# MLP up projection: the high weights meet low and high tokens in one 512-column product, and VectorE adds the halves

## The reference, cut to what matters

```python
D_MODEL = 1024
D_FF = 4 * D_MODEL

def squared_relu_mlp(x, w_up, w_down):
    return jnp.square(jax.nn.relu(x @ w_up)) @ w_down

def first_block(...):
    for layer in range(DEPTH):          # DEPTH = 2
        ...
        h = layer_norm(DEEPNORM_ALPHA * h + mix, ln1_g[layer], ln1_b[layer])
        h = layer_norm(DEEPNORM_ALPHA * h + squared_relu_mlp(h, w_up[layer], w_down[layer]),
                       ln2_g[layer], ln2_b[layer])
```

## Time and profile before

| | us |
|---|---|
| median of 3 runs | 1464.77 |
| lowest, highest | 1459.92, 1467.07 |
| profiled execution: span, first to last instruction | 1461.4 |

### The profile page before, as it was taken

One profiled execution on the slowest core, in us unless ns is written; L12 is line 12 of the kernel. 1 busy time (PEld: TensorE's weight loads), 2 busy tenths in 40 slices (PEclk: granted clock), 3 DMA queues, 4 the chain that ended last, 5 costly groups with the idle time before them and its releaser, 6 DMA issues.

```text
span 1461.4 us, 19665 instructions
## 1 busy us (share of the span) xinstructions
PE 1326.6 (91%) x6493; PEld 946.6 (65%) x6493; DVE 952.8 (65%) x2289; ACT 551.2 (38%) x1133; POOL 379.2 (26%) x384
## 2 busy tenths in 40 slices
PE   8999999999999999999998889787897989788888
PEld 6988999988988999977787535343343535343333
DVE  4687555564657555585785777776767777776755
ACT  4553544444545444454672222222222212222221
POOL 1104000000000000012642454335444354345440
PEclk9999999999999999999999999899999999999999
DMA  9615655535315555564403999999999999999997
GB/s 364 260 54 125 226 184 183 190 144 231 115 44 173 187 181 192 168 218 132 154 28 118 415 420 421 420 422 421 422 422 421 422 421 421 420 421 422 421 422 310
DMA packets 97535, 406.86 MB, mean 278 GB/s; under 512 B 6955, under 2 KB 44524, under 8 KB 60748
## 3 DMA queue, kind: packets, MB, share of 16 engines
q0 software_dynamic: 39552, 276.60, 46.0%
q1 hardware_dynamic: 57932, 129.60, 25.8%
HBM read 404.84 MB, written 1.07 MB: 278 GB/s over the span
## 4 chain that ended last, share of the span: by engine, by line
PE 50%; DMA 23%; issue 13%; DVE 10%; POOL 2%; ACT 2%; DVEq 0%; POOLq 0%; SPq 0%; ACTq 0%; PEldq 0%
DMA ring<-in_peer_uv,prob 20%; PE ps L688 13%; PE ps L689 12%; PE ps L690 12%; PE ps L841 6%; DMA uv_gain<-in_peer_uv,prob 2%; DMA ring<-in_peer_wq 1%; PE ps L815 1%; PE ps L877 1%; DVE prob L2417 1%; DVE prob L2405 1%; POOL small L1656 1%; PE ps L635 1%; DVE ring L2541 1%; DVE sco L2430 0%
## 5 line engine op out<-in xcount | busy, mean ns | idle before, releaser
L1876 DVE TENSOR_TENSOR w_low<-ring,w_high 128x1024 fp32r<-128x1024 f32 x140 | 165.2, 1222 | 151.3 <-ACT w_high L1220 150.8
L1220 ACT ACTIVATE w_high<-ring 128x1024 fp32r<-128x1024 f32 x142 | 142.7, 1052 | 171.8 <-PE ps L690 171.8
L688 PE MATMUL ps<-hT_high,w_high 128*128 128x256 f32 x512 | 145.0, 283 | 0.9 <-DVE hT_low L1869 0.9
L689 PE MATMUL ps<-hT_low,w_high 128*128 128x256 f32 x512 | 144.9, 283 | 0.0
L690 PE MATMUL ps<-hT_high,w_low 128*128 128x256 f32 x512 | 144.8, 283 | 0.0
L1471 ACT ACTIVATE prob<-prob 128x4 f32<-128x4 f32 (+2 forms) x67 | 13.8, 206 | 346.6 <-DVE prob L2541 346.6
L1459 ACT ACTIVATE sco<-const,prob 128x128 f32<-128x128 f32 x256 | 84.3, 392 | 151.7 <-DVE prob L2551 137.8
L841 PE MATMUL ps<-arena_v,sco 128*128 128x512 f32 x256 | 121.5, 619 | 18.6 <-ACT sco L1459 18.6
L1662 POOL TENSOR_SCALAR small<-small 128x1 f32<-128x1 f32 x8 | 4.3, 533 | 502.0 <-ACT arena_v L1252 502.0
L841 PE MATMUL ps<-ring,sco 128*128 128x512 f32 x192 | 102.4, 684 | 31.4 <-ACT sco L1459 31.4
L841 PE MATMUL ps<-arena_u,sco 128*128 128x512 f32 x256 | 115.7, 601 | 8.3 <-ACT sco L1459 8.3
(11 more groups left out here) (446 smaller groups left out, 3083.8 us busy)
## 6 DMA issues: line engine op xcount, KB each, us to landing
ring<-in_w_up SPq DMA_DIRECT2D x32, 1024.0 KB, 5.5
ring<-in_w_down SPq DMA_DIRECT2D x32, 1024.0 KB, 4.9
qkring<-in_qk_a SPq DMA_DIRECT2D x8, 1024.0 KB, 7.1
qkring<-in_qk_b SPq DMA_DIRECT2D x8, 1024.0 KB, 4.8
ring<-in_peer_wq SPq DMA_DIRECT2D x8, 1024.0 KB, 9.2
ring<-in_w_in SPq DMA_DIRECT2D x8, 860.0 KB, 5.5
ring<-in_w_out_a SPq DMA_DIRECT2D x4, 1024.0 KB, 15.8
ring<-in_v_b SPq DMA_DIRECT2D x4, 1024.0 KB, 7.2
```

What stands on the lines that cost most here:

```text
L688: pe.matmul(dst, a[0], b[0], start=start, stop=False, skip_group_check=True)
L689: pe.matmul(dst, a[0], b[1], start=False, stop=False, skip_group_check=True)
L1220: sc.activation(w_split[pair][0][:, part], ring[:, slot, part], ACT.Copy)\
L1876: ve.tensor_tensor(w_split[pair][1][:, part], ring[:, slot, part], w_split[pair][0][:, part].bitcast(F32), ALU.subtract)\
```

## The change

1. `hT_low` and `hT_high` become the two halves of one buffer, `hT_both`, at the same place in memory.
2. PSUM banks 4 to 7 become one tensor, `ps_up`; `ps[4]` to `ps[7]` are its slices. Each piece's up now takes two banks, one for each block of 128 hidden units: banks 4 and 5 for b = 0, 6 and 7 for b = 1.
3. In `up`, high weights times low tokens and high weights times high tokens are one matmul of 512 moving columns, which fills a bank: the low tokens' part in columns 0 to 255, the high tokens' in 256 to 511. Low weights times high tokens is added to the second half with a 256-column matmul. A group of three matmuls is now two.
4. ACT, after `up_ready`, first copies the first halves of the two banks into `relu` (a Copy in place of the Relu), and only then splits weights. DVE adds the second halves onto that, then computes max(x, 0)·x into `act_sq` with one scalar_tensor_tensor, signals `act_squared`, and then makes the weights' low halves. ACT makes `act_high` as a copy of `act_sq` after its weight split; DVE ends with `act_low` as before.
5. In the last step `final_split` now stands behind ACT's wait for `up_ready` and its copy.

```diff
-            hT_low = split("hT_low", [P, NB, S])
-            hT_high = split("hT_high", [P, NB, S])
+            hT_both = split("hT_both", [P, 2, NB, S])
+            hT_low, hT_high = hT_both[:, 0, :, :], hT_both[:, 1, :, :]
...
-        ps = [ctx.enter_context(nc.psum_tensor(f"ps{i}", [P, HALF], F32)) for i in range(8)]
+        ps = [ctx.enter_context(nc.psum_tensor(f"ps{i}", [P, HALF], F32)) for i in range(4)]
+        ps_up = ctx.enter_context(nc.psum_tensor("ps_up", [P, 4, HALF], F32))
+        ps += [ps_up[:, i, :] for i in range(4)]
...
-                        last = product(ps[4 + b][:, fb * S:(fb + 1) * S], [x[:, at:at + P] for x in w_split[pair]],
-                                       [x[:, c, :] for x in (hT_high, hT_low)], start=(c == 0), stop=(c == NB - 1))
+                        high, low = (x[:, at:at + P] for x in w_split[pair])
+                        pe.matmul(ps_up[:, 2 * b + fb, :].rearrange("p (a s) -> p a s", a=2), high, hT_both[:, :, c, :],
+                                  start=(c == 0), stop=False, skip_group_check=True)
+                        last = pe.matmul(ps_up[:, 2 * b + fb, S:2 * S], low, hT_high[:, c, :], start=False,
+                                         stop=(c == NB - 1), skip_group_check=True)
...
+                    sc.wait_ge(sem("up_ready"), count.take("up_ready"))
+                    sc.activation(relu[:, b, :].rearrange("p (f s) -> p f s", f=2), ps_up[:, 2 * b:2 * b + 2, 0:S], ACT.Copy)\
+                        .then_inc(sem("relu_ready"), 1)
                     if first:
-                        split_high(2 * b + 1, 0, "up_ready")
+                        split_high(2 * b + 1, 0)
                     elif more:
-                        split_high(2 - 2 * b, 1, "up_ready")
+                        split_high(2 - 2 * b, 1)
                     else:
                         final_split()
-                        sc.wait_ge(sem("up_ready"), count.take("up_ready"))
-                    sc.activation(relu[:, b, :], ps[4 + b][:, :], ACT.Relu).then_inc(sem("relu_ready"), 1)
-                    sc.wait_ge(sem("relu_ready"), count.take("relu_ready"))
-                    sc.activation(act_high[:, b, :], relu[:, b, :], ACT.Square).then_inc(sem("act_high"), 1)
+                    sc.wait_ge(sem("act_squared"), count.take("act_squared"))
+                    sc.activation(act_high[:, b, :], act_sq[:, b, :], ACT.Copy).then_inc(sem("act_high"), 1)
...
+                    ve.wait_ge(sem("relu_ready"), count.take("relu_ready"))
+                    pre = relu[:, b, :].rearrange("p (f s) -> p f s", f=2)
+                    then(ve.tensor_tensor(pre, ps_up[:, 2 * b:2 * b + 2, S:2 * S], pre, ALU.add))
+                    then(ve.scalar_tensor_tensor(out=act_sq[:, b, :], in0=relu[:, b, :], scalar=0.0, in1=relu[:, b, :],
+                                                 op0=ALU.max, op1=ALU.mult))
+                    ve.sem_inc(sem("act_squared"), 1)
                     if first:
                         split_low(2 * b + 1, 0)
...
-                    ve.wait_ge(sem("relu_ready"), count.take("relu_ready"))
-                    then(ve.tensor_tensor(act_sq[:, b, :], relu[:, b, :], relu[:, b, :], ALU.mult))
                     ve.wait_ge(sem("act_high"), count.take("act_high"))
```

More of the change, by code:

```diff
@@ L1387, in out_and_mlp @@
                 grow_residual()
-                with count.loop(N_CHUNK // 2 - 1, up_ready=2, relu_ready=2, w0_used=2, raw0_landed=16, raw1_landed=16,
+                with count.loop(N_CHUNK // 2 - 1, up_ready=2, act_squared=2, w0_used=2, raw0_landed=16, raw1_landed=16,
                                 raw2_landed=16, raw3_landed=16):
@@ L2095, in out_and_mlp @@
                 step(0, first=True)
-                with count.loop(N_CHUNK // 2 - 1, w_high=8, relu_ready=2, act_high=2, v_chain=2):
+                with count.loop(N_CHUNK // 2 - 1, w_high=8, relu_ready=2, act_high=2, v_chain=4):
                     step(1)
```

## The result

| | before | after |
|---|---|---|
| median, us | 1464.68 | 1469.49 |
| mean of 18 and 20 executions (standard error), us | 1463.7 (0.6) | 1469.5 (0.5) |
| profiled execution, span, us | 1461.4 | 1470.7 |

The ratio is **1.0043**, 95% interval 1.0032 to 1.0054 (1.0040 by the two means): the change makes the kernel about 6 us slower. The means leave out disturbed executions (4107.86 and 6595.08 us among the 20 before, which the median of 1464.68 counts, and in the experiments one of 2627 us before and one of 1641 us of e9). I had forecast 1465.0 and a shift of +0.2 us. What lies around a span is 1.8 us in every execution (the profiled one: 1472.5 against 1470.7).

The account below looks back on a forecast made before the run. PE was taken to bound the kernel, busy throughout both MLP windows. Terms of -4.9, 0, 0 and +5.1 us summed to +0.2 us, taking the median from 1464.8 to 1465.0 us; range 1460.0 to 1470.0.

Parts of the forecast that it names:

- Part 2: A step of the MLP loop: the down behind each up hides the new DVE and ACT work; cost 0.
- Part 3: First piece of each MLP: the longer chain to act_low stays covered by 0.2 us; cost 0, at worst 0.3 us.
- Part 4: Last piece of each MLP: nothing covers the chain, PE waits 2.5 us for act_low; +5.1 us for both.
- Part 1: The up matmuls: a group falls from 359.4 to 349.8 ns, saving 9.6 ns in each of 512, 4.9 us.
- the lower bound: Smallest expected saving in the up matmuls: 6.7 ns per group, 3.4 us, with the joined matmul at 232.9 ns.
- 1.3 us by my estimate from its rule: Rival for the up matmuls: only 2.5 ns fixed part saved per dropped matmul, giving 1468.6 us; chance 0.07.
- The clock: Rival: PE's clock falls in the new end gaps, 1.8 us per fall, 1466.8 or 1468.6 us; chance 0.25.
- a wait of PE is paid in full: In the MLPs, where PE is always busy, any wait of PE lengthens the kernel; the sum charged 2.5 us each.
- the last of the signs of failure: The forecast fails if the end gaps set off longer lower-clock stretches in the stages behind them; no size given.
- the rival with two falls: A clock fall in the end gap of both MLPs, giving 1468.6 us; one or two falls had chance 0.25.
- the 0.5% that I gave 0.87: Whole kernel: the time stays within about 0.5% (7.3 us), what a measurement can tell from no change; chance 0.87.

Follow-up runs that it names:

- e9: The changed kernel with 12 extra matmuls, results unread, filling PE's wait at the end of each MLP; mean 1465.6 us, ratio 1.0012 to before.
- e8: The changed kernel itself, unaltered, timed again on one chip beside its filled versions; mean 1468.9 us, ratio 1.0034 to before.
- e10: The changed kernel with 6 extra matmuls, results unread, half filling PE's wait at the end of each MLP; mean 1466.3 us, ratio 1.0019 to before.
- e2: The kernel before with only the final split moved late, three matmuls per group and the Relu kept; mean 1468.8 us, ratio 1.0040 to before.
- e3: The changed kernel with 12 extra unread matmuls in each end wait, first timing, on another chip than the changed kernel's; mean 1465.7 us, ratio 1.0019 to before.
- e1: The changed kernel with the final split put back ahead of the waits on ACT and DVE; mean 1462.4 us, ratio 0.9995 to before.
- e11: The kernel of e1 with three of the second last piece's matmuls moved ahead of the wait for act_ready; mean 1461.8 us, ratio 0.9993 to before.
- e5: The kernel of e1 with six of the second last piece's matmuls moved ahead of the wait for act_ready; mean 1462.3 us, ratio 0.9997 to before.

## Why the prediction was wrong

**Right.** What bounds the kernel, and that only the fixed part of a matmul can be saved. Part 2: PE busy for 120.00 of 120 us, ups and downs without a wait for `w_low`. Part 3: no wait of PE at the first piece (`act_low` ends at 155.88, 0.3 us before PE wants it at 156.15; the forecast was 0.2). Part 4: one wait of PE in each MLP, 12 matmuls after the last up, with the final low halves right ahead of `act_low`; that it cancels what the loops win was the core of the forecast, and it does, and takes 2.1 us more (5.8 against 3.7).

**Part 1, mis-sized.** 9.6 ns a group was 6.5: 3.3 us instead of 4.9 over 512 groups. I had chosen the down's 230.0 ns because it stands next to the up in time. The nearer row by kind was the output projection's 232.9, where tokens are an operand as well; it gave 3.4 us as the lower bound. That this is close to the 3.3 us measured is luck: the joined matmul takes 236.1 ns, 3.2 more than the row, and the 256-column one behind it 116.8, 3.0 less than the 119.8 that I had kept. By stages the loops win 3.7 us, since the downs run a shade faster too. The Trainium skill ("TensorE: Matmul & The Clock Gate", "Back-to-back issue gap") would have had 1.3 us by my estimate from its rule; the fixed parts of 23 and 10 ns above the columns (236.1 - 213.3, 116.8 - 106.7) don't agree with its 2.5.

**Part 4, mis-sized.** 2.5 us each was 3.1 and 2.7: 5.8 instead of 5.1 us. Of it 0.1 us each is the hand-over from DVE to PE, and 0.4 us at the first MLP is DVE, which starts the low halves at 315.08 though `act_sq` ended at 314.57 and the first high half at about 314.1. It does so in every trace of the changed kernel, filled or not, at the first MLP and in none at the second. Each time it starts 0.06 us behind the end of ACT's second high half (315.02 in this trace), though by the code it waits only for the first; why, I don't know.

**The clock, the step that failed.** I named it as a rival at 0.25 and left it out of the sum. The sum took "a wait of PE is paid in full" to mean its length and no more. The runs show that a wait that PE spends idle costs more than one of the same length that it spends on matmuls: 3.3 (0.9) us for the two together, e8 less e9. Without it the sum by the stages is -3.7 + 5.8 = +2.1 us, and that is what the filled kernels have, +1.8 (0.7) and +2.9 (0.7). With it the sum is +5.4 us; measured are +5.8 (0.8) and, in e8 itself, +5.1 (0.8). The longer stretches at the lower clock were the last of the signs of failure that the prediction named. I had the row for it: a gap of 1.81 us followed by a clock of 0.57. Against it stood one gap of 1.75 us without a fall, and I let two rows count as a coin toss for gaps half as long again. What I priced at 1.8 us per fall was right in size for a short one (1.5), and short of a long one (2.8).

**The range.** 1469.5 lies inside the range, 0.5 us below its end, and +0.43% inside the 0.5% that I gave 0.87. The range reached that far because it took in the rival with two falls (1468.6), not because of the forecast: +5.8 (0.8) us is clear of the noise, and of +0.2.

**Still open.** A fall behind the first wait explains 1.5 or 2.8 us and none was seen behind the second, so the traces locate only part of the mean 3.3 us. The traces of e8 and e9 differ by 3.7 us: 1.5 us in the last downs of the first MLP, 1.6 between the MLPs, 0.7 ahead of the first one. The 1.6 us is a fall of 3.4 us near 427 to 430, which all three traces of unfilled kernels have and the filled ones lack. But the kernel before has one there too (6.8 us from 421), and so have the four traces with the early split, whose waits are 0 to 0.9 us (from 421 to 425). So it isn't shown that the wait brings this one; whether a wait shifts when later falls come isn't settled.

The mean clocks of whole executions don't settle it either. By clock and span an execution has 98.8 (2.0) us at the lower clock in e8, 92.6 (2.3) in e9, and 92.2 in e10 without one execution that has 217. That goes A's way. But e2 has 88.8 (1.3) and its kernel before 87.7 (1.1), hardly more. Most of this time, 77 to 96 us of it in each trace, lies behind the MLPs, where it costs little: 19 us more of it in e3's trace than in e2's go with 0.8 us more from there to the end.

## What to carry to other kernels

Joining matmuls that share their stationary operand saves only the fixed part, here 6.5 ns of 359 per group; count that before paying for it elsewhere. When a step is reordered for a loop, its last turn needs a sum of its own: the piece with nothing behind it to hide the chain is where the gain went. And a wait of PE of 2 to 3 us behind dense matmuls can cost more than its length: here four of eight traced waits had a fall with them, of 1.5 to 2.8 us each. Shorten the wait (e1: all of the loss came back), or fill it (e9: 3.3 us of 5.1 came back).

## What the runs showed of the hardware that I had not expected

At the ends of the MLPs PE's clock went to its lower level (matmuls 427 ns apart, 1.2 GHz) at waits of 2.9 us (the first MLP of three traces) and 2.0 us (e2, second MLP). The fall began between 0.7 us before the end of the wait (after) and 1.5 us behind it (e8). At waits of 0.9 us (e1), 1.2 and 1.6 us (e10), 2.0 us (e2, first MLP) and 2.58 us (the second MLP of three traces) there was none.

The length of the gap alone doesn't decide. Elsewhere some gaps of PE come back in each of the twelve traces. At one of 0.8 us, between 420 and 430 us, 8 of 12 traces have a fall; at one of 1.7 us, between 106 and 111, 7 of 12; at the one of 1.8 us behind the second MLP (2.3 and 2.5 us in e11 and e5), 9 of 12; at one of 1.75 us, some 6 us behind the first MLP, none. The rows show the gap of 0.8 us in the changed kernel, with a matmul at the lower clock (0.63 us long) behind it, and the gap of 1.75 us in the kernel before, with one at the full clock:

```profile
429.88 0.51 PE L646 MATMUL ps_up<-val,probT 128*128 128x64 f32 x2 [0.82 <-ACT probT L1288]
...
432.32 0.63 PE L691 MATMUL ps<-w_low,hT_both 128*128 128x512 f32 x1
```

```profile
329.66 1.06 PE L586 MATMUL ps<-const,h 128*128 128x128 f32 x8 [1.75 <-DVE v_low L1890]
330.48 0.48 PE L688 MATMUL ps<-v_high,hT_high 128*128 128x512 f32 x1
```

Ahead of the first, PE was not dense: it was busy for 2.44 of the 4.00 us up to 430.00. The Trainium skill ("TensorE: Matmul & The Clock Gate", "Why this matters for your kernels") advises against gaps over about 3 us; in these traces every fall ahead of 700 us came at a shorter gap. Twelve matmuls into a bank that nobody reads are faster than waiting: 1465.6 against 1468.9 us.
